# Hyena layer: filter matmuls between the k-steps of the input projection, two PSUM bank sets in turn, the last forward leaves ahead of the prompt's inverse leaves, and the first convolution job begun beside the last group

## The reference

```python
def hyena_filters(L, lp):
    ...
    hdn = jnp.sin(fr * (feat @ lp['hy_w1'] + lp['hy_b1']))   # three such layers, 64 wide
    filt = (hdn @ lp['hy_w4']).reshape(L, 2, HY_ORDER, HY_WIDTH)
    return filt * window[:, None, None, :] * lag_mask
def mixer_hyena(h, lp):
    u = dwconv1d(h @ lp['w_in'], lp['hy_short_w']) + lp['hy_short_b']
    v, x1, x2 = ...                                          # 1024 channels each
    resp = filt_f[:, 0] + jnp.conj(filt_f[:, 1])             # spectrum of the filters
    z = v
    for o, gate in enumerate((x1, x2)):
        conv = irfft(rfft(z, 2 * L) * resp[:, o], 2 * L)[:, :L]
        z = gate * (conv + z * bias[o])
    return z @ lp['w_out']
```

## Time and profile before

| | |
|---|---|
| median of 3 runs | 4835.26 us (4834.79 to 4835.74) |
| profiled execution | 4830.18 us, span of its instructions 4828.4 us |
| busy share of the span | PE 86%, DVE 51%, POOL 24%, ACT 21% |
| mean granted clock of TensorE | 0.915 of 2.4 GHz |
| chain that ended last | PE 70%, DVE 18%, DMA 3%, issue 3% |

### The profile page before, as it was taken

One profiled execution on the slowest core, in us unless ns is written; L12 is line 12 of the kernel. 1 busy time (PEld: TensorE's weight loads), 2 busy tenths in 40 slices (PEclk: granted clock), 3 DMA queues, 4 the chain that ended last, 5 costly groups with the idle time before them and its releaser, 6 DMA issues.

```text
span 4828.4 us, 50522 instructions
## 1 busy us (share of the span) xinstructions
PE 4173.2 (86%) x21784; PEld 3474.9 (72%) x21784; DVE 2454.5 (51%) x2598; ACT 1018.6 (21%) x1384; POOL 1176.3 (24%) x586
## 2 busy tenths in 40 slices
PE   6799888788679999999778989986665799999998
PEld 3488777777468888888656777775554688888886
DVE  1465154555236444454375546458884364444543
ACT  1234211122122111111232333311101221111112
POOL 1211223333133222222320000012221332222224
PEclk8799699999789999999878898898887899999998
DMA  9511000000210111111112221232121111111111
GB/s 352 198 45 38 27 1 1 1 1 1 92 31 28 40 40 37 40 37 41 66 51 62 69 86 54 85 140 81 61 101 67 30 31 37 40 40 37 40 38 61
DMA packets 253813, 280.41 MB, mean 58 GB/s; under 512 B 7941, under 2 KB 217814, under 8 KB 249079
## 3 DMA queue, kind: packets, MB, share of 16 engines
q1 hardware_dynamic: 253592, 277.18, 17.2%
HBM read 219.48 MB, written 57.67 MB: 57 GB/s over the span
## 4 chain that ended last, share of the span: by engine, by line
PE 70%; DVE 18%; DMA 3%; issue 3%; ACT 2%; POOL 2%; SPq 1%; POOLq 0%; DVEq 0%; ACTq 0%
PE PS L590 52%; DVE piece L1470 8%; PE PS L1538 5%; DVE piece L1019 3%; DMA piece<-in_l_ada_w 2%; PE PS L990 2%; PE PS L991 2%; DVE piece L516 2%; PE PS L1708 2%; PE PS L986 2%; PE PS L702 1%; DVE piece L509 1%; DVE piece L1406 1%; ACT piece L1759 0%; PE PS L1004 0%
## 5 line engine op out<-in xcount | busy, mean ns | idle before, releaser
L590 PE MATMUL PS<-piece,piece 128*128 128x512 f32 (+1 forms) x13824 | 2753.8, 361 | 154.1 <-POOL piece L534 97.6
L590 PEld LDWEIGHTS PS<-piece,piece 128*128 128x128 f32 x13824 | 2312.6, 191 | 598.2 <-issue 146.6
L573 POOL TENSOR_TENSOR piece<-piece,piece 128x1024 fp32r<-128x1024 f32 (+1 forms) x204 | 500.1, 2453 | 2504.7 <-ACT piece L567 2504.7
L1538 PE MATMUL PS<-piece,piece 128*128 128x256 f32 x1920 | 440.1, 392 | 160.7 <-POOL piece L2016 140.8
L1406 DVE SCALAR_TENSOR_TENSOR piece<-piece,piece,piece 128x1024 f32<-128x1024 f32 x352 | 534.9, 1520 | 12.6
L1538 PEld LDWEIGHTS PS<-piece,piece 128*128 128x128 f32 x1920 | 376.0, 197 | 222.2 <-issue 167.4
L1426 DVE SCALAR_TENSOR_TENSOR piece<-PS,piece,piece 128x1024 f32<-128x1024 f32 x224 | 187.8, 880 | 415.4 <-PE PS L590 415.4
L567 ACT ACTIVATE piece<-piece 128x1024 fp32r<-128x1024 f32 (+1 forms) x204 | 205.0, 1006 | 674.4 <-PE PS L590 634.3
L1019 DVE TENSOR_TENSOR piece<-piece,PS 128x512 f32<-128x512 f32 x288 | 185.4, 684 | 249.6 <-PE PS L991 195.1
L1403 DVE TENSOR_SCALAR piece<-piece,piece 128x1024 f32<-128x1024 f32 x44 | 35.8, 814 | 482.4 <-ACT piece L1367 482.4
L1470 DVE TENSOR_TENSOR piece<-piece 128x512 f32<-128x512 f32 (+2 forms) x168 | 176.4, 1050 | 28.3 <-DMA piece<-hyena_tokens 13.3
(11 more groups left out here) (206 smaller groups left out, 3810.4 us busy)
## 6 DMA issues: line engine op xcount, KB each, us to landing
piece<-in_l_ada_w SPq DMA_DIRECT2D x24, 2048.0 KB, 17.9
piece<-in_l_ffn_up SPq DMA_DIRECT2D x88, 512.0 KB, 3.7
piece<-in_l_w_in SPq DMA_DIRECT2D x44, 512.0 KB, 5.5
piece<-in_l_ffn_down SPq DMA_DIRECT2D x48, 384.0 KB, 3.0
filters_s<-piece SPq DMA_DIRECT2D x8, 2176.0 KB, 6.6
piece<-filters_s SPq DMA_DIRECT2D x8, 2176.0 KB, 9.1
hyena_tokens<-piece SPq DMA_DIRECT2D x24, 640.0 KB, 4.5
piece<-hyena_tokens SPq DMA_DIRECT2D x12, 1280.0 KB, 5.6
```

What stands on the lines that cost most here:

```text
L573: eng.tensor_tensor(LO[i % 2][0][:, 0:n], RAW[i % 2][:, 0:n], HI[i % 2][1][:, 0:n], ALU.subtract)\
L590: m = eng.matmul(PS[:, bank + b, 0:n], w, x[:, a:a + n], start=first and n_ == 0, stop=last and n_ == 2)
L1538: m = eng.matmul(PS[:, bank, o * HC:(o + 1) * HC], M[i][o], rhs[i], start=i == 0, stop=i == 1)
```

## The change

1. Filter work moves between k-steps. A table `behind[k]` on PE places it after the product of k-step k. The mlp matmuls of groups 0, 2, 4 follow k-steps 3 to 7. Taps of filter f: four follow k-step 7 of group 6 + 2f, six follow k-steps 0 to 2 of the group after it. The twelve leaves of filter f follow k-steps 5 to 7 of group 8 + 2f, where the taps of f + 1 begin; so a leaf now comes one group later than before. ACT mixes leaf copies and windows, DVE takes the s taps before the convolution of the group and the p taps and the tree after it. The sums and differences are now made in slices of two rows.
2. Group n uses banks 0 to 2 or 3 to 5 by its parity, for the product and for its turning, which stands after k-step 5 (6 where there are leaves) of the next group.
3. A leaf goes through one of four buffers `LEAF` to HBM with its own store, twelve for a filter, and `RED` is doubled. To make room the weight ring has one landing buffer (`raws` = 1), so load n + 2 waits for the halves of n + 1.
4. Part 2 no longer waits for part 1 as a whole. `first_loads` fetches z and the filters of job 0 from within the last groups, DVE runs the tree of job 0 before the convolution of group 23, and PE does five of job 0's forward leaves before the last turning.
5. In every job s6 and s7 stand ahead of the inverse leaves of p.

```diff
-            ring = weight_ring(r, n_t)
+            ring = weight_ring(ring_at, n_t, 1)
...
-                    if i >= 2:
-                        eng.wait_ge(self.po.sem, self.po.at("lo", i - 2))
-                        eng.wait_ge(self.ac.sem, self.ac.at("hi", i - 2))
+                    if i >= raws:
+                        eng.wait_ge(self.po.sem, self.po.at("lo", i - raws))
+                        eng.wait_ge(self.ac.sem, self.ac.at("hi", i - raws))
...
-            EXTRA = {0: ("mlp", 0), 2: ("mlp", 1), 4: ("mlp", 2)}
-            for f in range(len(JOBS)):
-                EXTRA[6 + 2 * f], EXTRA[7 + 2 * f] = ("tap", f), ("leaf", f)
+            LEAVES_FROM = 5
+            BEFORE_TURN = 8
+            MLP_AT = {0: 0, 2: 1, 4: 2}
+            TAP_AT = {6 + 2 * f: f for f in range(len(JOBS))}
+            LEAF_AT = {8 + 2 * f: f for f in range(len(JOBS))}
...
+                    behind = {k: [] for k in range(KD)}
+                    if n in MLP_AT:
+                        for c in range(5):
+                            behind[3 + c].append((mlp, MLP_AT[n], c))
+                    if n in LEAF_AT:
+                        for q, (g, l) in enumerate(ALL_LEAVES):
+                            behind[LEAVES_FROM + q // 4].append((leaf, LEAF_AT[n], g, l))
+                    if n in TAP_AT:
+                        behind[KD - 1] += [(tap, TAP_AT[n], "s", b) for b in TAP_ORDER["s"][:4]]
+                    if n - 1 in TAP_AT:
+                        for q, (g, b) in enumerate([("s", b) for b in TAP_ORDER["s"][4:]] + [("p", b) for b in TAP_ORDER["p"]]):
+                            behind[q // 2].append((tap, TAP_AT[n - 1], g, b))
+                    turn_at = KD - 2 if n in LEAF_AT else KD - 3
...
-                        if n:
-                            eng.wait_ge(acW.sem, acW.at("p", n - 1))
+                        if n >= 2:
+                            eng.wait_ge(acT.sem, acT.at("e", n - 2))
...
-                            m = product(eng, 0, (wh[:, k, :], wl[:, k, :]), (HH[:, k], HL[:, k]), k == 0, k == KD - 1)
+                            m = product(eng, 3 * (n % 2), (wh[:, k, :], wl[:, k, :]), (HH[:, k], HL[:, k]), k == 0, k == KD - 1)
+                            if k == KD - 1:
+                                m.then_inc(*ring.pe.did("used", n))
+                        if k == turn_at and n == n_t:
+                            first_leaves(eng)
+                        for f, *args in behind[k]:
+                            f(*args)
+                        if k == turn_at and n:
+                            turn(n - 1)
...
+                    buf, stored, count = leaf_slot(f, g, l)
+                    if count:
+                        eng.wait_ge(stored, count)
+                    eng.activation(row(buf, 0, n), PS[:, small_bank(acF[g], step, f), 0:n * HC], ACT.Copy).then_inc(*acF[g].did(step, f))
...
+                    if n in TAP_AT:
+                        taps("s", TAP_AT[n])
+                    if n == n_t - 1:
+                        start_tree(eng, 0)
...
-                        if l == N_BANKS["s"]:
-                            if k == 0:
-                                eng.wait_ge(s_iv, 16)
-                            for lp in LEAVES["p"]:
-                                inverse("p", lp, k)
...
-                    for l in LEAVES["s"]:
-                        inverse("s", l, k)
+                    if k == 0:
+                        eng.wait_ge(s_iv, 16)
+                    for g in "ps":
+                        for l in LEAVES[g]:
+                            inverse(g, l, k)
```

More of the change, by code:

```diff
@@ L1586, in mixer_hyena @@
[L1586 to L1603 removed]
+                peF[g] = steps("pe_filter_" + g, [f"h{l}" for l in LEAVES[g]] + ["hx"], len(JOBS))
@@ L1666, in _, with mlp @@
             def _(eng):
-                for n, (kind, f) in slots():
+                def mlp(f, c):
+                    if f == 0 and c == 0:
+                        eng.wait_ge(s_mlp, 80)
+                    kk = EMB if f == 0 else FFN64
+                    src = FEAT if f == 0 else HD
+                    i = 5 * f + c
+                    if f:
+                        eng.wait_ge(acM.sem, acM.at("sin", i - 5))
+                    wait_bank(eng, veM_, "arg", i)
+                    eng.matmul(PS[0:FFN64, small_bank(veM_, "arg", i), :], MLPW[0:kk, f, :], src[0:kk, c * 512:(c + 1) * 512],
+                               start=True, stop=True).then_inc(*peM.did("t", i))
@@ new lines, in tap @@
+                def tap(f, g, b):
+                    c, order = JOBS[f]
+                    eng.wait_ge(s_c, 48 * (c + 1))
+                    base = 0 if g == "s" else 2 * NS
+                    wait_bank(eng, veF[g], f"k{b}", f)
+                    bank = small_bank(veF[g], f"k{b}", f)
+                    for u in range(2):
+                        at = 2 * b + u
+                        m = eng.matmul(PS[:, bank, u * HC:(u + 1) * HC], HD[0:FFN64, base + at * P:base + (at + 1) * P],
+                                       W4[0:FFN64, 2 * (at // T_OF[g]) + order, :], start=True, stop=True)
+                    m.then_inc(*peX[g].did(f"tap{b}", f))
@@ L1731, in _, with window @@
                 eng.wait_ge(veZ.sem, veZ.end())
-                for n, (kind, f) in slots():
+                def window(f, g, b):
+                    if b == 0 and f:
+                        eng.wait_ge(veF[g].sem, veF[g].at(leaves_made[g], f - 1))
+                    for at in (2 * b, 2 * b + 1):
+                        m = eng.activation(KB[g][:, at, :], DELTA, ACT.Exp, scale=WIN[g][:, 0, at:at + 1], bias=WIN[g][:, 1, at:at + 1])
+                    m.then_inc(*acX[g].did(f"win{b}", f))
@@ new lines, in leave @@
+                def leave(n):
+                    eng.wait_ge(peT.sem, peT.at("t", n))
+                    if n:
+                        eng.wait_ge(s_tok, 16 * n)
+                    eng.activation(STG, psum(3 * (n % 2), N).rearrange("p (t c) -> p t c", c=P), ACT.Copy).then_inc(*acT.did("e", n))
+                for n in range(n_t + 1):
+                    if n in TAP_AT:
+                        eng.wait_ge(s_c, 48 * (JOBS[TAP_AT[n]][0] + 1))
+                    if n == 6:
+                        eng.wait_ge(s_k, 64)
+                        eng.wait_ge(peM.sem, peM.end())
+                    if n and n not in LEAF_AT:
+                        leave(n - 1)
+                    leaves = ALL_LEAVES if n in LEAF_AT else []
+                    taps = [(g, b) for g in "sp" for b in TAP_ORDER[g]] if n in TAP_AT else []
+                    for q in range(max(len(leaves), len(taps))):
+                        if q == BEFORE_TURN and leaves:
+                            leave(n - 1)
+                        if q < len(leaves):
+                            leaf(LEAF_AT[n], *leaves[q])
+                        if q < len(taps):
+                            window(TAP_AT[n], *taps[q])
+                    if n in MLP_AT:
+                        f = MLP_AT[n]
+                        for i in range(5 * f, 5 * f + 4):
+                            eng.wait_ge(veM_.sem, veM_.at("clamp", i))
+                            eng.activation(HD[0:FFN64, (i % 5) * 512:(i % 5 + 1) * 512], RED[i % 2][0:FFN64, :], ACT.Sin).then_inc(*acM.did("sin", i))
```

407 lines of the change are left out of this document (219 added, 188 removed).

## The result

The changed kernel takes 4690.4 us (median of four runs, 4688.5 to 4696.2), the kernel before 4835.5 beside it: a ratio of 0.9701, 95% interval 0.9684 to 0.9717. The forecast was 4686, its range 4652 to 4745. The profiled execution took 4689.3 us, its span is 4687.5, 140.9 less than before.

| stretch | before | predicted | after |
|---|---|---|---|
| span's start to group 6 (mlp groups) | 2580.6 | -26 | 2554.0 (-26.7) |
| group 6 to the end of group 23, pairs | 620.9 | -81 | 548.6 (-72.3) |
| from there to job 1's tree, seam | 49.0 | -23 | 28.7 (-20.3) |
| job 1's tree to part 3's first product, s6 and s7 | 455.7 | -19 | 434.1 (-21.7) |
| sum | | -149 | -141.0 |

What follows compares the result with a forecast made beforehand. Part 1 hangs on PE and part 2 on DVE. Terms -81 - 26 - 23 - 19 = -149 take the profiled 4830.2 to 4681; the median stands 5.1 higher: 4686 us, range 4652 to 4745.

Steps and rivals of the forecast that it cites:

- Pairs, -81: Part 1, group 6 to the end of group 23: PE work, remaining waits and clock loss sum to 539.7 us against 620.9.
- the 29.4 of the sum: PE's remaining waits for DVE in the pairs: 1.8 us before tap 5 seven times, 2.1 before the leaves eight times.
- The prediction's 2.15: Delay in us of DVE's first slice additions when POOL's low half of the weights runs beside them in the pairs.
- mlp groups, -26: Groups 2 to 6: mlp pieces beside k-steps make two groups take 36.6 us, saving 12.3 and 13.4.
- the first layer gains nothing wherever it stands: Group 0's mlp: it waits for its tables wherever it stands, so its gain is 0.
- Seam, -23: End of group 23's work to job 1's tree: 26 us instead of 49, between -26 and -8.
- s6 and s7, -19: Part 2: these leaves moved ahead of p's inverse leaves cut DVE's waits by 18.8 us, bounds 0 to -36.
- a clock of 0.5 in the odd groups: Sign of being wrong: the profile's clock rows show PE's granted clock at 0.5 in part 1's odd groups.
- the rival's 81: Part 1: clock stays at 1.2 GHz through the interleaved stretch, 10.1 us a pair, 81 in all, giving 4757; chance 15%.
- No wait remains: Pairs and part 2: POOL misses the adds and the tree is early, giving 4640; chance 6%.
- DVE sets the pace: Pairs: POOL visits or late windows and copies add 3.5 to 6 us a pair, giving 4714 to 4734; chance 10%.
- Leaf copies: Part 1: ACT's leaf copies wait for their stores, making the kernel slower, 4880 at 15 us landing time; chance 3%.

Runs made afterwards that it cites:

- experiment 2: Changed kernel with POOL's first low half of a weight held back until DVE's third s slice: 4669.4 us; second also held until the tree ends: 4647.4 us.
- experiment 6: Version with both POOL low halves held back, mlp layers at groups 1, 3, 5: 4650.6 us; sine wait also moved: 4648.2; layers at 1, 2, 4: 4641.6; unchanged: 4646.3.
- experiment 4: Changed kernel with job 0's tree behind group 23's convolution on DVE and its first leaves behind PE's last turning: 4697.3 us.
- experiment 5: Kernel before with only DVE's order changed, the eight s taps, their sum and difference ahead of the group's convolution: 4888.9 us, ratio 1.0114.
- experiment 3: Changed kernel with all ten taps in one block behind k-step 7: 4712.4 us; the same with 128-row taps, upper 64 rows zero: 4697.2 us.

## Why the prediction was right

**Pairs, -81, measured -72.3.** The mechanism held at each place: the releasers are DVE's L1879 and the tree, and POOL is what makes both late (experiment 2). By terms: waits 24.1 us (10.5 at taps, 13.6 at leaves, seven each) for the 29.4 of the sum. The clock was mis-sized: the stretches at 1.2 GHz last 3.4 us six times (five behind tap waits, one behind the longest wait for leaves) and 13.8 once, 34.2 in all, which costs half of that, 17 us; the step took 2.4 us eight times, which costs 9.6. The rest is work: with waits and clock gone (experiment 2) PE takes 507 us from group 6 to the end of group 23 (2556.9 to 3064.8, less 1.0 of wait), 6 more than the 500.7 added up from products and taps at their own pace; a k-step between other work takes 1.95 us, not 1.76. 24 + 17 + 507 = 548. So the sum had the waits 5 us too long and the clock and the work 7 and 6 too short, and came closer than its terms did. No run takes the two bank sets, the later leaves or the single landing buffer out alone; what each of these is worth is not shown.

The rule of the Trainium skill that was weighed, SBUF — State Buffer (Who interferes with whom), is what the runs show: an addition of two SBUF operands loses 2.17 us to a POOL instruction of 2.36, the multiplication that reads PSUM nothing. The prediction's 2.15 came from the convolution's row, and was right by size; it placed it on the slices' additions, and it fell on the bias. (The section counts more than the prediction's "only" allows, namely DVE instructions in a two-port mode too; the sum does not use that.) The trace of before could have told: in the very pair of the earlier trace rows the bias of s takes 0.41 us, that of p, beside POOL's second low half at 2930.34, 2.33.

```profile
2909.40 0.41 DVE L1827 TENSOR_TENSOR piece<-piece,piece 1x256 f32<-1x256 f32 x1
...
2930.64 2.33 DVE L1827 TENSOR_TENSOR piece<-piece,piece 1x256 f32<-1x256 f32 x1
...
2930.34 2.35 POOL L573 TENSOR_TENSOR piece<-piece,piece 128x1024 fp32r<-128x1024 f32 x1 [35.89 <-ACT piece L567]
```

**mlp groups, -26, measured -26.7.** The timeline of PE, from the turning in group 2 to that in group 4, gives 36.65 us for the 36.6 of the sum, and no wait for DVE's six steps is left:

```profile
2494.72 1.31 PE L1736 MATMUL PS<-piece,piece 128*128 128x128 f32 x10
2495.78 1.98 PE L590 MATMUL PS<-piece,piece 128*128 128x512 f32 x9
2497.70 1.07 PE L1700 MATMUL PS<-piece,piece 64*64 64x512 f32 x2
...
2531.37 1.31 PE L1736 MATMUL PS<-piece,piece 128*128 128x128 f32 x10
```

The sum is made up otherwise than forecast: the turning of the even group does not wait 1.4 us; PE waits 0.58 for ACT a little later, and matmul pairs (1.0 us for 0.88) and single k-steps (1.93 for 1.76) take the rest. No run undoes this part alone. That the first layer gains nothing wherever it stands holds for the time, but not for its reason: behind group 1 it no longer waits for its tables, and other waits take the gain back, all but some 5 us that the times do not show (experiment 6).

**Seam, -23, measured -20.3.** Each date comes 1 to 3 us after the one predicted, counted from the last product's end at 3102.6: z issued at -14.0 (-15), tree's end at 7.0 (5.8), job 1's z issued at 19.1 (17), its tree at 28.7 (26). The last turning runs at 1.2 GHz (2.25 us), which the step had at full speed. The early tree and leaves are worth 3 us together (experiment 4); that the early load of z carries the rest is argued from that, not tried alone.

**s6 and s7, -19, measured -21.7.** The times between the products of successive jobs fell by 5.3, 3.9, 1.0, 0.8, 5.2 and 3.8 us (jobs 1 to 6), for 3.9, 3.9, 1.7, 0.7, 3.9 and 3.9: the wait that the step put at 1.2 is 0.0 to 0.6 in jobs 1, 2, 5 and 6. The gates of jobs 3 and 4 became late, as forecast.

**Total.** The sum put the profiled execution at 4681; it took 4689.3. The median stood 5.1 above the profiled execution before and 1.1 after, which the prediction could not know, so 4686 is nearer to 4690.4 than its working was.

**The rivals.** The clock did not stay low: 0.97 over part 1. But one of the prediction's own signs of being wrong, a clock of 0.5 in the odd groups, did show, for 3.4 us in five of seven pairs and 13.8 in one; that is 15 of the 17 us above, small beside the rival's 81. The Trainium skill's TensorE: Matmul & The Clock Gate (A second HAM failure mode: psum-queue depth-cycling) lays such swings on cycling through banks with short pauses; here the cycling alone does nothing (1.00 with the pauses gone, same banks). The falls stand behind pauses, but not behind every pause: in the changed kernel behind six of seven of 1.5 us before the half-height tap 5, behind none of six of 1.7 to 1.8 us before the full-height leaves, and behind the one of 3.1 us there. *No wait remains* (4640) is what experiment 2 made of it, 4647. *DVE sets the pace* did not come: a pair takes 64.7 us, where the sum's terms give 63.9, not 3.5 to 6 more, though DVE is behind both waits. Leaf copies never made PE wait, and ACT shows no wait for the stores, which land in 2.0 us.

## What to carry to other kernels

Where two engines share something, a small instruction can pay for a large one beside it: look for the same line with two durations, and move the cheap engine's work to where the other reads PSUM, waits, or is not waited for. Fill a wait with work that has another limit, but then look at what is late next: here two waits on POOL gave 43 us more, nearly a third of what the whole change gave. An order that belongs together with other moves can show a loss when it is tried alone, as in experiment 5.

## What the runs showed of the hardware

A matmul with 64 rows takes the time of one with 128 (sixteen records 3.96 us and 3.94, experiment 3), but behind a pause of 3.4 to 3.5 us the clock stayed at its lower level for 13.6 us of half-height matmuls and products, and for 6.0 when the missing rows were filled with zeros. And one wait does not have one price: in the changed kernel seven waits of 1.5 us before the same tap were followed by 3.4 us at 1.2 GHz five times, by 13.8 once and by none once. The last two kinds, as windows:

```profile
3028.60:3042.40 13.80, 13.80 (x34) 9.70 (x34) 8.67 (x13) 0.00 (x0) 0.00 (x0) 0.51 0.00 1
2964.00:2978.00 14.00, 13.43 (x62) 10.45 (x63) 12.93 (x18) 0.00 (x0) 0.00 (x0) 1.00 0.11 32
```
